# Rearranged joins and projection halves, and SwiGLU weights used once for two activation parts, in a hybrid decoder kernel

## The reference, cut to what matters

```python
x = x + rwkv7_time_mix(x, ...)          # norm, six token mixes, LoRAs, r/k/v projections,
                                        # delta-rule scan over 16 heads, head norm, gate, w_o
x = x + swiglu_ffn(x, f_norm_g[0], f_w_gu[0], f_w_down[0])
k_sh, v_sh = shared_kv(x, kv_norm_g, w_kv, k_norm_g, cos, sin)
x = x + dilated_mixer(x, k_sh, v_sh, cos, sin, b_norm_g, b_w_q, b_q_norm_g, b_w_o)
x = x + swiglu_ffn(x, f_norm_g[1], f_w_gu[1], f_w_down[1])

def swiglu_ffn(x, norm_g, w_gu, w_down):          # D_FF = 2816
    h = rms_norm(x, norm_g)
    gate, up = jnp.split(h @ w_gu, 2, axis=-1)
    return (jax.nn.silu(gate) * up) @ w_down
```

## Time and profile before

| what | value |
|---|---|
| median of 3 runs | 1081.63 us |
| profiled execution: time, span | 1084.32 us, 1082.5 us |
| TensorE matmuls busy | 997.9 us (92%), 7192 |
| VectorE, ScalarE, GpSimd busy | 61%, 36%, 5% |
| matmul group hsp x wsp (gate/up) | 265.0 us, 2112 |
| matmul group hkq x wpj (projections) | 216.4 us, 1152 |
| granted TensorE clock, mean | 0.962 |
| DMA | 137.41 MB, 127 GB/s over the span |

### The profile page before, as it was taken

How to read it: one execution, slowest core, us unless ns; L and a number is a source line. 1 busy time by engine, 2 the same in 40 slices (tenths; PEclk the granted TensorE clock), 3 DMA queues, 4 the chain that set the end, 5 groups by cost and what they waited for, 6 DMA issues and landing times.

```text
span 1082.5 us, 17968 instructions
## 1 busy us (share of the span) xinstructions
PE 997.9 (92%) x7192; PEld 873.4 (81%) x7192; DVE 657.3 (61%) x1196; ACT 393.7 (36%) x566; POOL 54.8 (5%) x52
## 2 busy tenths in 40 slices
PE   5979989999887999999898999999998789999998
PEld 3768678687675999999787888888888449999997
DVE  6774774757735655555485777677777235555553
ACT  1301303013013433443345555456555323433331
POOL 0000000000000000000011110111101000000000
PEclk9999999999967999999999999999999889999999
DMA  9310130500503656666366544444454106666561
GB/s 299 113 56 2 63 106 1 161 7 1 157 1 90 183 175 184 192 195 185 96 242 176 143 120 135 129 121 136 122 144 135 45 1 189 194 188 186 174 179 54
DMA packets 194978, 137.41 MB, mean 127 GB/s; under 512 B 7261, under 2 KB 185949, under 8 KB 194794
## 3 DMA queue, kind: packets, MB, share of 16 engines
q1 hardware_dynamic: 194922, 136.62, 42.8%
HBM read 135.55 MB, written 1.05 MB: 126 GB/s over the span
## 4 chain that ended last, share of the span: by engine, by line
PE 57%; issue 28%; DVE 9%; POOL 3%; DMA 1%; ACT 1%; SPq 0%; POOLq 0%; DVEq 0%; ACTq 0%
PE wide L402 35%; PE bank L402 21%; DVE work L1030 3%; POOL gsm L1448 3%; DVE work L1229 1%; DVE work L1033 1%; DVE work L1236 1%; DVE x L1030 1%; DMA gain<-in_a_norm_g 1%; DMA ring<-in_w_kv 0%; DVE wsp L1030 0%; PE bank L412 0%; DVE work L1218 0%; DVE fhn L1033 0%; SPq L369 0%
## 5 line engine op out<-in xcount | busy, mean ns | idle before, releaser
L402 PEld LDWEIGHTS wide<-hsp,wsp 128*128 128x128 f32 x2112 | 263.7, 195 | 6.7 <-DVE hsp L1030 3.6
L402 PE MATMUL wide<-hsp,wsp 128*128 128x256 f32 x2112 | 265.0, 286 | 2.8 <-DVE hsp L1030 2.8
L402 PE MATMUL bank<-wpj,hkq 128*128 128x384 f32 x1152 | 216.4, 342 | 21.6 <-DVE wpj L1030 19.9
L402 PEld LDWEIGHTS bank<-wpj,hkq 128*128 128x128 f32 x1152 | 199.8, 189 | 30.2 <-DVE wpj L1030 24.0
L1030 DVE TENSOR_TENSOR wsp<-ring,wsp 128x1024 fp32r<-128x1024 f32 (+1 forms) x88 | 151.0, 1756 | 36.1 <-ACT wsp L801 36.1
L801 ACT ACTIVATE wsp<-ring 128x1024 fp32r<-128x1024 f32 (+1 forms) x88 | 130.0, 1484 | 27.2 <-PE wide L402 27.2
L1030 DVE TENSOR_TENSOR am<-sg,wide 128x256 f32<-128x256 f32 x44 | 18.5, 421 | 146.1 <-ACT sg L801 146.1
L1030 DVE TENSOR_TENSOR wpj<-ring,wpj 128x1536 fp32r<-128x1536 f32 x48 | 84.2, 1755 | 33.2 <-ACT wpj L801 33.2
L402 PE MATMUL bank<-work 64*64 64x64 f32 (+5 forms) x1200 | 79.1, 249 | 22.4 <-DVE work L1229 14.8
L402 PE MATMUL bank<-wsp,asp 128*128 128x512 f32 x396 | 98.1, 392 | 0.0
L402 PEld LDWEIGHTS bank<-work 64*64 64x64 f32 (+3 forms) x1200 | 62.8, 150 | 38.7 <-DVE work L1229 20.1
(11 more groups left out here) (160 smaller groups left out, 996.5 us busy)
## 6 DMA issues: line engine op xcount, KB each, us to landing
ring<-in_f_w_gu SPq DMA_DIRECT2D x88, 512.0 KB, 5.8
ring<-in_w_kv SPq DMA_DIRECT2D x96, 256.0 KB, 3.5
ring<-in_f_w_down SPq DMA_DIRECT2D x44, 512.0 KB, 3.7
ring<-in_b_w_q SPq DMA_DIRECT2D x48, 256.0 KB, 3.5
wmix<-in_a_w_k SPq DMA_DIRECT2D x4, 1024.0 KB, 7.7
wmix<-in_a_w_r SPq DMA_DIRECT2D x4, 1024.0 KB, 10.1
wmix<-in_a_w_v SPq DMA_DIRECT2D x4, 1024.0 KB, 6.6
wmix<-in_a_w_o SPq DMA_DIRECT2D x4, 1024.0 KB, 5.2
```

The costliest lines, as they stand in the source:

```text
L402: return pe.matmul(o, a, b, start=start, stop=stop)
```

## The change

- *Start:* the norm gain of the time mix is no longer loaded as a broadcast of its own; it is a 14th row of the small table `rows` and is applied per column block when the turned tiles leave PSUM. Row tile 1 is scaled by ScalarE. The gate LoRA comes first. GpSimd clears `work` and `Us`.
- *First join:* in the last group ScalarE and VectorE split the first SwiGLU weights, chunk 0 of the output is squared and turned inside the group, and residual adds go between the steps of the norm.
- *SwiGLU:* gate and up have a PSUM bank each. A high weight block meets both activation parts in one matmul of 512 columns (256 of each part); its low block meets the high part, 256 columns. ScalarE copies the second 256 columns out, VectorE adds them to the first. The next `gu_hi` stands ahead of the silu. The halves of `wsp` are exchanged.
- *Projection halves:* the high weights of both row tiles come first and wait only for ScalarE's part; `half_hi(p, 3)` stands ahead of the squares.
- *Second join:* `half_lo(0, 0)` stands before the residual adds; tile 0 is split before tile 1 is scaled; the query turning stands inside step 0.
- *Third join:* the output projection is spread over the last step's softmax, the norm of row tile 0 over its last product.

Cut to its core:

```diff
             def gate_up(f, b, b_free=True):
                 pe.wait_ge(S("dve_gu_lo"), f + (base + 1))
                 if b_free:
-                    pe.wait_ge(S("dve_act"), f + (base - 1))
+                    pe.wait_ge(S("dve_us"), f + (base - 1))
                 for m_ in range(2):
-                    o = bank[4 + b][:, m_ * T:(m_ + 1) * T]
+                    o = gu_bank(b, m_)
                     for k in range(KT):
-                        for n, (sw, sh) in enumerate(PASSES):
-                            m = mm(o, gus[b][:, sw, k, m_, :], hparts[:, sh, k, :],
-                                   k == 0 and n == 0, k == KT - 1 and n == 2)
-                m.then_inc(S("pe_gu"), 1)
+                        mm(o, gus[b][:, 0, k, m_, :], hparts[:, :, k, :], k == 0, False)
+                        m = mm(o[:, 0:T], gus[b][:, 1, k, m_, :], hparts[:, 0, k, :], False, k == KT - 1)
+                    m.then_inc(S("pe_gu"), 1)
...
+                def sides(f, b, used=True):
+                    for m_ in range(2):
+                        act.wait_ge(S("pe_gu"), f * 2 + (2 * base + m_ + 1))
+                        if used:
+                            act.wait_ge(S("dve_us" if m_ else "dve_gs"), f + base)
+                        A(side[:, m_, :], gu_bank(b, m_)[:, T:2 * T], ACT.Copy).then_inc(S("act_side"), 1)
...
-                    silu(f, b)
+                    sides(f, b, used or layer > 0)
                     if more:
                         gu_hi(f + 2, b, n2)
+                    silu(f, b)
                     dn_hi(f + 1, 1 - b, n, used)
...
                 def product(f, b, later=True):
+                    for m_, (total, done) in enumerate(((gsum, "dve_gs"), (usum, "dve_us"))):
+                        dve.wait_ge(S("act_side"), f * 2 + (2 * base + m_ + 1))
+                        if later:
+                            dve.wait_ge(S("act_sg" if m_ == 0 else "dve_act"), f + base)
+                        tt(total, gu_bank(b, m_)[:, 0:T], side[:, m_, :], ALU.add).then_inc(S(done), 1)
                     dve.wait_ge(S("act_sg"), f + (base + 1))
-                    step(tt(am[:, :], sg[:, b, :], bank[4 + b][:, T:2 * T], ALU.mult))
+                    step(tt(am[:, :], sg[:, b, :], usum, ALU.mult))
...
                 def project_half(u, tiles=range(RT)):
                     what, h = u // 2, u % 2
-                    pe.wait_ge(S("dve_w_lo"), p * UNITS + (u + 1))
+                    pe.wait_ge(S("act_w_hi"), p * UNITS + (u + 1))
                     for r in tiles:
                         for k in range(KT // 2):
-                            for n, (sh, sw) in enumerate(PASSES):
-                                m = mm(bank[r][:, 0:384], src[:, sh, h * (KT // 2) + k, r * P:(r + 1) * P],
-                                       wpj[:, h, sw, k * 384:(k + 1) * 384], ...
+                            for sh in range(2):
+                                mm(bank[r][:, 0:384], src[:, sh, h * (KT // 2) + k, r * P:(r + 1) * P],
+                                   wpj[:, h, 0, k * 384:(k + 1) * 384], h == 0 and k == 0 and sh == 0, False)
+                    pe.wait_ge(S("dve_w_lo"), p * UNITS + (u + 1))
+                    for r in tiles:
+                        for k in range(KT // 2):
+                            m = mm(bank[r][:, 0:384], src[:, 0, h * (KT // 2) + k, r * P:(r + 1) * P],
+                                   wpj[:, h, 1, k * 384:(k + 1) * 384], False, h == 1 and k == KT // 2 - 1)
                         m.then_inc(S("pe_half"), 1)
...
+                if not A:
+                    scores(0)
+                    scores(1)
...
+                    product_out(0, 0, range(KT - 1))
+                    turn_p(0)
+                    weigh(0)
+                    product_out(0, 1, range(4))
+                    turn_p(1)
+                    product_out(0, 1, range(4, KT - 1))
+                    weigh(1)
...
+                    product_out(1, 0, range(KT - 1))
...
+                    turn_rows((fhn, "dve_hn"), RT, [0])
+                    product_out(1, 1, range(KT))
+                    return
...
                 product(NF - 1, 1)
+                if layer == 0:
+                    half_lo(0, 0)
                 for i in range(4):
                     dve.wait_ge(S("pe_sums"), 4 * layer + i + 1)
...
+            pool.wait_ge(S("dve_mix"), 3)
+            pool.memset(work[:, 0:8 * 512], 0.0).then_inc(S("pool_zeros"), 1)
```

More of the change, by code:

```diff
@@ L402, in mm, with turn_rows @@
                 return pe.matmul(o, a, b, start=start, stop=stop)
-            def turn_rows(src, n0):
-                for r in range(RT):
+            def turn_rows(src, n0, tiles=range(RT)):
+                for r in tiles:
                     pe.wait_ge(S(src[1]), n0 + r + 1)
@@ L622, in group @@
                 next_keys(3)
+                if not ahead:
+                    turn_output(NGRP, [0])
                 pe.wait_ge(S("act_uu"), it * 2 + 2)
@@ L699, in _, with turn_queries @@
             turn_rows((ahn, "dve_ahn"), 0)
-            for r in range(RT):
+            def turn_queries(r):
                 pe.wait_ge(S("dve_ahn"), RT + r + 1)
@@ L801, in A, with squares @@
                 return act.activation(o, i, f, **k)
-            def squares(n, scratch, rows_ready=None, count=0):
-                for r in range(RT):
+            def squares(n, scratch, rows_ready=None, count=0, tiles=range(RT)):
+                for r in tiles:
                     if n == 0:
@@ L838, in square_output, with group @@
                 A(osq[:, c * T:(c + 1) * T], oc[:, c * T:(c + 1) * T], ACT.Square).then_inc(S("act_osq"), 1)
-            def group(it, behind=True):
+            def group(it, behind=True, ahead=True):
                 if behind:
@@ L885, in group @@
                 for c in range(2):
+                    if c == 1 and not ahead:
+                        square_output(NGRP, 0)
                     if c == 1:
@@ L1076, in scale_rows, with norm @@
                 stt(o[:, r, :], x[:, r, :], small[:, 4 + r:5 + r], gain[:, gi, :], ALU.mult, ALU.mult).then_inc(S(name), 1)
-            def norm(n, o, name, gi, count):
-                for r in range(RT):
+            def norm(n, o, name, gi, count, tiles=range(RT)):
+                for r in tiles:
                     dve.wait_ge(S("act_ss"), n * RT + r + 1)
@@ L1230, in turn_blocks @@
                                   Uc[:, 4 * h:4 * h + 4, :].rearrange("p u t -> p (u t)")).then_inc(S("dve_T"), 1)
+                if not behind:
+                    dve.wait_ge(S("pool_zeros"), 2)
                 for u in range(8):
@@ L1268, in group @@
                         tt(bv, bank[7], vT, ALU.mult)
+                if not ahead:
+                    gu_lo(0, 0, 0)
                 for h in range(2):
@@ L1344, in _, with rows_lo @@
             ffn(0)
-            norm(2, ahn, "dve_ahn", 0, 32)
-            for r in range(RT):
-                scale_rows(ahn2, 1, 32, r, "dve_ahn")
-            def rows_lo(parts, b0, n0):
-                for i in range(4):
+            def rows_lo(parts, b0, n0, tiles):
+                for i in tiles:
                     dve.wait_ge(S("act_aturned"), n0 + i + 1)
```

277 lines of the change are left out of this document (174 added, 103 removed).

## The result

| | before | changed |
|---|---|---|
| median of 4 executions, us | 1082.16 | 1040.19 |
| lowest, highest | 1081.52, 1084.69 | 1039.32, 1040.87 |
| ratio, 95% interval | | 0.9608 [0.959, 0.9625] |
| profiled execution, span | 1084.32, 1082.5 | 1039.32, 1037.5 |
| mean granted clock | 0.962 | 0.971 |

The change saves 42.0 us, 3.9%. Two later measurements of the same pair of kernels give ratios of 0.962 [0.9597, 0.9643] and 0.9641 [0.9597, 0.9686]. The forecast was 1045 with 1030 to 1057: the result is inside, and 4.8 us faster than the forecast. The time came from these stages. The starts that bound them are the first matmul of the named group in the two timelines, and the differences add up to the 45.0 us between the spans.

The account below looks back on a forecast made before the run. It took the kernel to be bound by TensorE: its matmul time in SwiGLU, its waits elsewhere. Terms -7.3 - 16.0 - 2.5 - 2.0 + 0.5 - 9.2 = -36.5 from 1081.6 gave 1045 us, range 1030 to 1057.

Parts of the forecast that it names:

- SwiGLU, -7.3: 44 SwiGLU tiles: a 512- and a 256-column matmul replace three short ones, 5.58 against 5.75 us a tile; -7.3 us.
- little or nothing: Rival in SwiGLU: the matmul pair saves little or nothing, other terms stand; 1050 to 1052 us, chance 12%.
- nearly bare: Rival in SwiGLU: the pair streams halfway or more to 0.320 us; 1025 to 1035 us, chance 9%.
- Cost of the split sum, 0: SwiGLU tiles: the added ScalarE copies and VectorE adds stay hidden under TensorE's work; cost 0.
- Projection halves, -16.0: Attention steps: high-weight matmuls first remove TensorE's waits for VectorE's low parts; -16.0 us, bounds -8 and -16.7.
- The third rival: VectorE's rotation chain holds each attention step (8 lost), joins give half (5 lost); 1053 to 1062 us, chance 15%.
- Start, -2.5: Kernel start: without the gain's DMA wait, first LoRA matmul at 15.6 instead of 17.20; -2.5 us, bounds -1 and -4.3.
- Second join, +0.5: Between SwiGLU and attention: adds end 2.2 later, projection starts earlier, step 0 gets more work; +0.5 us, bounds -3 and +3.
- Third join, -9.2: Attention's end: output projection fills softmax waits, a norm goes under its last product; -9.2 us, bounds -6 and -11.9.
- First join, -2.0: Before the first SwiGLU: earlier chunk 0 product, adds and norm, less a low part's delay; -2.0 us, bounds +1 and -4.8.
- Four groups, 0: Stage from group 0's first matmul to the last level's product: no change forecast, 0 us.
- The signs named beforehand: Marks to check: SwiGLU tile 8.33 us, attention steps 34.2 to 34.6, third join about 45 rather than 54.

Follow-up runs that it names:

- e3: Changed kernel with each bank's eight 512-column gate/up matmuls first, then its eight 256-column ones, instead of by turns; 1039.56 us.
- e1: Changed kernel with gate/up as three 256-column matmuls per block again, banks and side work kept; 1047.91 us, ratio 0.9695.
- e6: Changed kernel with ScalarE's old order at the first projection halves (copy, square, copy, square, then high part), TensorE's new order kept; 1047.98 us.
- e8: Changed kernel with the attention's output projection after the last softmax again, rest of the third join as changed; 1049.81 us.
- e9: Changed kernel with four edits: matmuls grouped by width, first SwiGLU low part later, half 0's low part behind residual adds, output-weight load later; 1035.46 us, ratio 0.9589.
- its control: The changed kernel unaltered, run beside the version of four edits on its chip; 1041.12 us, ratio 0.9641.
- e7: Changed kernel with both TensorE's pass order and ScalarE's order at the projection halves as before; 1066.54 us.

## Why the prediction came out right

The result is inside the range, and by the steps that were forecast, but two terms were mis-sized, and a third came near by two errors that cancelled.

- **SwiGLU, -7.3: the mechanism right, the size 2.1 too large.** The steady tile gives 44 x 0.112 = 4.9, the two stages 5.2. The sum of the single spacings (0.229 + 0.120 = 0.349) left out most of the turn from one width to the other, some thirty of them per tile; e3 shows it. The bounds held, and the rivals "little or nothing" and "nearly bare" are out by e1 and by 0.3525. By the rule of the Trainium skill (TensorE: Matmul & The Clock Gate, Back-to-back issue gap, N/2.4 + 2.5 ns, which the page gives for the isolated gap) a pair would have saved one start, 2.5 ns; it saved 6.9, and with the widths grouped 12. The measurement decides: in this stream, with a weight load ahead of each matmul, a start costs more than the rule's 2.5 ns.
- **Cost of the split sum, 0: right.** VectorE 5.24 and ScalarE 3.95 per tile against my 5.3 and 4.0, and e1 has them without loss.
- **Projection halves, -16.0: the mechanism right, the size 6 too small, and that is the forecast's error.** I took the waits from the matmul rows, 1.52 + 1.01, where the weight loads waited 1.76 + 1.25. A matmul's end in these rows is modelled, some 0.25 us behind the point where the engine could go on, so the idle before the next is too short; my bound of -16.7, just the idle of the window, had the same fault and was no bound. Counted as I counted, with the right lengths, the waits are 7 x 1.76 + 6 x 1.25 = 19.8. The 22.1 of the stage are six steps of 3.11, 18.7; the last one up to its scores, 1.8, since only the fourth half's wait lies in it; and 1.6 in the first half of step 1, which stood at the lower clock level in the kernel before (6.00 us) and not in the one after (4.40). That last part is clock and no wait, and it is luck: e3 with the new orders has the slow half too. And I credited TensorE's order with nearly all of it: by e6 it gives 2.58 of the 3.11, and the last 0.53 needs ScalarE's.
- **The third rival, waits that change their name:** did not happen in the steady steps, but e6 has it at 0.54 a step, and the slack is less than the 0.3 us of my schedule: in the changed kernel the last rotated queries are done at 667.52, and the first weight load that needs them starts at 667.61. In step 0 the waits did change their name: the kernel before ends it with 1.37 for the queries and 2.70 for the low part, the one after with 0.97 and 1.88, both for the queries.
- **Start, -2.5:** -2.93, with the first LoRA matmul at 15.15 and not 15.6. Two more executions of the changed kernel reach group 0 at 38.60 and 39.40 instead of 38.19, so against the one trace of before this is 1.7 to 2.9.
- **Second join, +0.5:** +0.70; it is no shorter, as said. The adds end 5.8 us behind the start of the last down product instead of 3.6, as forecast (+2.2), the projection starts 14.25 instead of 15.56 behind it (-1.3, forecast -1.7), and step 0, with the query turning now inside, takes 33.88 instead of 31.87.
- **Third join, -9.2:** -10.05, the number nearly right and its parts not. I had 6.1 us of softmax idle, 1.5 of clock and 1.5 of the norm by tiles. The traces have 4.9 less idle in all and 5.2 less busy time for the same 158 matmuls, nearly all of it clock (0.86 before, 0.98 after); and e8 gives 10.0 for the product's place alone, which leaves nothing for the norm. That the two errors cancelled is luck.
- **First join, -2.0:** -3.27. The low part is felt as forecast (0.90 at 297.65), and the first tile's lower clock stayed. Of the 3.27, 2.0 is busy time for one matmul record less (granted clock 0.74 over the join instead of 0.68) and 1.3 is idle time; so, as far as the two traces tell, the part that is order and not clock is smaller than my 2.0. I have no run that splits the product from the adds.
- **Four groups, 0:** -2.13 with the same instructions. e9 and its control differ by 2.7 in the same stage (255.1 and 257.8), on both sides of the 257.0 of the kernel before, so this need not be an effect of the change.

Between the profiled executions the sum misses by 8.5: halves 6.1, groups 2.1, first join 1.3, third 0.9, start 0.4, less SwiGLU 2.1 and the second join 0.2. Between the medians it misses by 4.8, since the profiled execution of before lay 2.2 above its median and the one after 0.9 below, and the median before was 0.5 lower when I forecast.

The signs named beforehand: the tile was to be 8.33 and is 8.39, inside 8.2 to 8.45; steps were to be 34.2 to 34.6 and are 33.73, under my band; the third join was to take 45 instead of 54, counted from the last key turning, and took 44.1 (42.9 from the last scores, as in the table).

## What to carry to other kernels

Read a TensorE wait at the weight loads, or from the distance between two starts of a repeating step; the idle before a matmul row and the busy share hide part of each wait. When two engines' orders serve one saving (here TensorE's passes and ScalarE's copies), undo them one by one and together before crediting either: what each costs when undone (1.31, 0.53) says nothing of what it brings alone (2.58, 1.80). Where an engine waits for a chain of others, fill it with work whose inputs have long been ready: an output projection inside a softmax was worth 10 us, twice what all SwiGLU tiles gave, and about half of it is busy time of the same matmuls, which then ran at a higher granted clock.

## What the runs showed of the hardware

- **Turning between widths costs TensorE time.** 16 + 16 matmuls of 512 and 256 columns took 5.64 us by turns and 5.56 grouped per bank, 5.0 ns a pair. Whether the 512 columns lie in one run or in two of 256 made no difference (5.64 both).
- **A GpSimd memset holds up a VectorE cast.** A VectorE cast of 0.43 us took 3.79 when a GpSimd memset of 3.51 started in the same hundredth, a copy 0.47 instead of 0.18 beside a second one. The Trainium skill (SBUF — State Buffer, section SBUF: two separate sides) has GpSimd and a VectorE instruction in a mode that uses two ports take an exclusive lock on a shared pair of ports for a whole instruction; the trace agrees, by 3.36 us more on a cast beside a memset of 3.51. Whether the memset was held up too is not shown.
- **Executions of the same instructions differ by the granted clock.** They reached the first gate/up matmul between 334.4 and 340.2 us (the last in e7, which is the same up to there); 28 small matmuls of the first join took 6.07 or 6.08 us in thirteen traces and 3.24 in one, where the granted clock over them is 1.00 instead of 0.50. What decided it stays open.
